# Second layer's sample attention written out with two buffers a side and scores one batch ahead; index key pages fetched in the feed-forward stage before

## What is computed

```python
def dsa_select(qi, wi, q_pos, ki, k_pos, k_sel):
    s = jnp.einsum('bqhd,bkd->bqhk', qi, ki).astype(jnp.float32) * (IDX_DIM ** -0.5)
    score = jnp.einsum('bqhk,bqh->bqk', jax.nn.relu(s), wi.astype(jnp.float32)) * (IDX_HEADS ** -0.5)
    score = jnp.where(k_pos[None, None, :] <= q_pos[None, :, None], score, -jnp.inf)
    _, idx = lax.top_k(score, k_sel)
...
    s = jnp.einsum('bqgrd,bqkgd->bqgrk', qg, k_sel).astype(jnp.float32) * (HEAD_DIM ** -0.5)
    p = jax.nn.softmax(jnp.where(valid[:, :, None, None, :], s, -jnp.inf), axis=-1)
    o = jnp.einsum('bqgrk,bqkgd->bqgrd', p.astype(v_sel.dtype), v_sel)
```

## Time and profile before

| | |
|---|---|
| median of 3 runs | 2020.21 us (2020.12 to 2026.99) |
| the profiled execution, its own time | 2022.86 us |
| its span, first to last instruction | 2021.0 us |
| mean granted TensorE clock | 0.928 |
| PE busy | 1752.4 us (87%) |
| DVE busy | 893.4 us (44%) |
| ACT busy | 563.9 us (28%) |
| POOL busy | 103.8 us (5%) |
| HBM read, written | 190.57 MB, 8.82 MB |

### The profile page before, as it was taken

One profiled execution on the slowest core, in us unless ns is written; L12 is line 12 of the kernel. 1 busy time (PEld: TensorE's weight loads), 2 busy tenths in 40 slices (PEclk: granted clock), 3 DMA queues, 4 the chain that ended last, 5 costly groups with the idle time before them and its releaser, 6 DMA issues. The chain is left out here.

```text
span 2021.0 us, 30720 instructions
## 1 busy us (share of the span) xinstructions
PE 1752.4 (87%) x11710; PEld 1431.7 (71%) x11718; DVE 893.4 (44%) x1662; ACT 563.9 (28%) x1087; POOL 103.8 (5%) x91
## 2 busy tenths in 40 slices
PE   5998798889889999999982596687779999999999
PEld 4786565455579988999772374454448999789987
DVE  4457354555352222322242779995444322222212
ACT  3322364233232211122131222453222322112211
POOL 1322012000000000000000022000000000000000
PEclk9999898999999999999986798797779899999999
DMA  5232302999422322332212120001553232223221
GB/s 172 74 120 78 121 1 86 373 374 342 140 73 69 83 79 78 84 83 78 81 39 53 50 86 21 22 1 46 160 143 85 63 83 78 78 73 81 80 74 63
DMA packets 176269, 200.73 MB, mean 99 GB/s; under 512 B 21546, under 2 KB 130794, under 8 KB 176170
## 3 DMA queue, kind: packets, MB, share of 16 engines
q1 hardware_dynamic: 171498, 193.12, 30.1%
q10 hardware_dynamic: 4592, 6.05, 0.9%
q0 software_dynamic: 80, 0.26, 0.0%
HBM read 190.57 MB, written 8.82 MB: 99 GB/s over the span
## 5 line engine op out<-in xcount | busy, mean ns | idle before, releaser
L206 PE MATMUL ps<-feat_lo,w_hi 128*128 128x288 f32 x1408 | 417.4, 296 | 8.5 <-DVEq L1850 8.5
L208 PE MATMUL ps<-feat_hi,w_hi 128*128 128x288 f32 x1408 | 417.2, 296 | 0.0
L207 PE MATMUL ps<-feat_hi,w_lo 128*128 128x288 f32 x1408 | 416.9, 296 | 0.0
L188 DVE TENSOR_TENSOR w_lo<-w_raw,w_hi 128x2048 fp32r<-128x2048 f32 x96 | 220.2, 2293 | 387.5 <-ACT w_hi L182 387.4
L182 ACT ACTIVATE w_hi<-w_raw 128x2048 fp32r<-128x2048 f32 x96 | 183.8, 1914 | 407.9 <-PE ps L214 357.7
L206 PEld LDWEIGHTS ps<-feat_lo,w_hi 128*128 128x128 f32 x1408 | 266.3, 189 | 9.8 <-DVEq L1850 9.8
L207 PEld LDWEIGHTS ps<-feat_hi,w_lo 128*128 128x128 f32 x1408 | 266.5, 189 | 0.0
L208 PEld LDWEIGHTS ps<-feat_hi,w_hi 128*128 128x128 f32 x1408 | 266.3, 189 | 0.0
L206 PE MATMUL ps<-w_lo,feat_hi 128*128 128x512 f32 (+1 forms) x448 | 181.0, 404 | 18.9 <-DVE p_xn L739 6.6
L208 PE MATMUL ps<-w_hi,feat_hi 128*128 128x512 f32 (+1 forms) x448 | 177.3, 396 | 0.0
L207 PE MATMUL ps<-w_hi,feat_lo 128*128 128x512 f32 (+1 forms) x448 | 177.1, 395 | 0.0
(11 more groups left out here) (276 smaller groups left out, 2376.7 us busy)
## 6 DMA issues: line engine op xcount, KB each, us to landing
s_vslot<-in_cache_l_v_dram SPq DMA_DIRECT2D x64, 512.0 KB, 6.6
s_kslot<-in_cache_l_k_dram SPq DMA_DIRECT2D x56, 512.0 KB, 6.7
w_raw<-in_w_gate_dram SPq DMA_DIRECT2D x44, 512.0 KB, 4.0
w_raw<-in_w_up_dram SPq DMA_DIRECT2D x44, 512.0 KB, 5.2
w_raw<-in_w_in_dram SPq DMA_DIRECT2D x18, 1024.0 KB, 5.3
w_raw<-in_w_down_dram SPq DMA_DIRECT2D x16, 1024.0 KB, 5.1
s_vslot<-in_cache_l_v_dram SPq DMA_DIRECT2D x64, 128.0 KB, 2.7
s_kslot<-in_cache_l_k_dram SPq DMA_DIRECT2D x56, 128.0 KB, 2.1
```

The source lines that it names most:

```text
L188: dve.tensor_tensor(self.K.w_lo[:, n % 2, :], self.K.w_raw[:, n % 2, :], self.K.w_hi[:, n % 2, :].bitcast(F32), ALU.subtract).then_inc(sel ...
L206: pe.matmul(out, lhs[0], rhs[1], start=start, stop=False)
L207: pe.matmul(out, lhs[1], rhs[0], start=False, stop=False)
L208: return pe.matmul(out, lhs[0], rhs[0], start=False, stop=stop)
```

## The change

There are two edits. First, the 64 index pages are fetched in `f0g1`, the second `gate_up` of layer 0, 5 or 6 behind each chunk's weight load on SyncE's queue; `kidx_pages` lives from there to the end of layer 1, with a semaphore that outlives the phase. `project` loses its `aside`. Second, layer 1 no longer calls `sample_attention` but a function of its own, `selected_attention`, whose batches are written out without loops. It has two buffers each for key pages, value pages, turned keys (all in `kt0`), queries, new keys and running sums, two pairs of score banks; the masks and the new values of all batches come with two DMAs at the start. TensorE turns the keys of batch b+2 and scores batch b+1 ahead of weighing batch b. Here is the diff, cut:

```diff
@@ project (pi: parts[:1])
-def project(nc, K, parts, tag, aside=None, side=None):
+def project(nc, K, parts, tag, side=None):
...
             for i, n in enumerate(tiles):
                 W.load_up_to(sp, n + 2)
...
-                if aside is not None:
-                    for j in range(DEC_BATCH * i // len(tiles), DEC_BATCH * (i + 1) // len(tiles)):
-                        aside(sp, j)
@@ gate_up
-def gate_up(nc, K, tag, act_hi, act_lo, first, n_chunks):
+def gate_up(nc, K, tag, act_hi, act_lo, first, n_chunks, pages=None):
...
         def _(sp):
+            if pages is not None:
+                total = DEC_BATCH * N_PAGES
+                for n in range(n_chunks):
+                    W.load_up_to(sp, first + n + 2)
+                    pages.load(sp, total * n // n_chunks, total * (n + 1) // n_chunks)
             W.load_up_to(sp, first + n_chunks + 2)
@@ IndexPages
-        self.landed = K.sem("kidx_pages_landed")
+        self.landed = nc.alloc_semaphore(name="kidx_pages_landed")
-    def load(self, sp, b):
+    def load(self, sp, first, last):
         K = self.K
-        for j in range(N_PAGES):
-            n = b * N_PAGES + j
+        for n in range(first, last):
             pid = sp.value_load(K.pages[0:1, n:n + 1], min_val=0, max_val=K.cache_l1_kidx.shape[0] - 1)
-            sp.dma_start(self.rows[:, b, j, :], K.cache_l1_kidx[ds(pid, 1), :, :]
+            sp.dma_start(self.rows[:, n // N_PAGES, n % N_PAGES, :], K.cache_l1_kidx[ds(pid, 1), :, :]
                          .rearrange("a k d -> (a k) d")).then_inc(self.landed, 16)
@@ ffn, two_layers
-                gate_up(nc, K, f"{tag}g{f}", act_hi, act_lo, gu, FH)
+                gate_up(nc, K, f"{tag}g{f}", act_hi, act_lo, gu, FH, pages if f == 1 else None)
...
-    ffn("f0", ffn0, next_gain=2)
+    second = ExitStack()
+    kidx_pages = IndexPages(nc, K, second)
+    ffn("f0", ffn0, next_gain=2, pages=kidx_pages)
...
-            with ExitStack() as idx:
-                kidx_pages = IndexPages(nc, K, idx)
-                project(nc, K, parts[:1], "pi", aside=kidx_pages.load)
-                score_keys(nc, K, top, sample_top, kidx_pages)
+            project(nc, K, parts[:1], "pi")
+            score_keys(nc, K, top, sample_top, kidx_pages)
...
-        sample_attention(
-            nc, K, "s1", ...)
+        selected_attention(
+            nc, K, K.cache_l1_k.rearrange("n k g d -> n k (g d)"), K.cache_l1_v.rearrange("n k g d -> n k (g d)"),
+            K.s_l1_v, fill_q1, ks, out1_fn, early)
@@ new: selected_attention
+    WIDTH, CHUNKS, UNITS = 256, 2, N_PAGES // 2
...
+        kslot, vslot = (sb(x, [P, 2, N_PAGES, WIDTH]) for x in ("kslot", "vslot"))
+        kt = K.kt0[:, 0:2 * 2 * CHUNKS * BANK].rearrange("p (s g c n) -> p s g c n", s=2, g=2, c=CHUNKS)
...
+        vnew = sb("vnew", [DEC_SEQ, DEC_BATCH, WIDTH])
+        masks = sb("masks", [DEC_SEQ, DEC_BATCH, KEYS], BF16)
...
+            def load_k(b, pages):
+                for j in range(N_PAGES):
+                    if b >= 2:
+                        sp.wait_ge(S["k_turned"], UNITS * (b - 2) + j // 2 + 1)
+                    sp.dma_start(kslot[:, b % 2, j, :], cache_k[ds(pages[j], 1), :, :].rearrange("a k d -> (a k) d"))\
+                      .then_inc(k_in[b % 2][j], 16)
+
+            def load_v(b, pages):
+                if b >= 2:
+                    sp.wait_ge(S["weighed"], b - 1)
+                for j in range(N_PAGES):
+                    sp.dma_start(vslot[:, b % 2, j, :], cache_v[ds(pages[j], 1), :, :].rearrange("a k d -> (a k) d"))\
+                      .then_inc(v_in[b % 2][j // 4], 16)
+
+            sp.dma_start(masks[:, :, :], K.mask_rows.rearrange("b q k -> q b k")).then_inc(S["rows_in"], 16)
+            sp.dma_start(vnew[:, :, :], new_v.rearrange("(b q) d -> q b d", b=B)).then_inc(S["rows_in"], 16)
+            now = ids(1)
+            load_k(1, now)
+            load_v(0, ids(0))
+            load_v(1, now)
+            for b in range(2, B):
+                now = ids(b)
+                load_k(b, now)
+                load_v(b, now)
...
+            for i in range(UNITS):
+                turn_k(0, i)
+            scores(0)
+            for i in range(UNITS):
+                turn_k(1, i)
+            for b in range(B):
+                if b + 1 < B:
+                    scores(b + 1)
+                if b + 2 < B:
+                    turn_k(b + 2, 0)
+                    turn_k(b + 2, 1)
+                turn_probs(b, 0)
+                if b:
+                    turn_o(b - 1)
+                if b + 2 < B:
+                    turn_k(b + 2, 2)
+                turn_probs(b, 1)
+                if b + 2 < B:
+                    turn_k(b + 2, 3)
+                weigh(b)
+            turn_o(B - 1)
...
+            for b in range(B):
+                if b + 2 < B:
+                    kt_out(act, b + 2, 0)
+                probs_out(b)
+                if b + 1 < B:
+                    exp(b + 1, 0)
+                if b + 2 < B:
+                    kt_out(act, b + 2, 2)
+                if b + 1 < B:
+                    exp(b + 1, 1)
+                    exp(b + 1, 2)
...
+            for b in range(B):
+                sums(b)
+                if b + 1 < B:
+                    shift(b + 1)
+                if b + 2 < B:
+                    kt_out(dve, b + 2, 1)
+                if b:
+                    finish(b - 1)
+                if b + 2 < B:
+                    queries(b + 2)
+                probs_out(b)
+                if b + 2 < B:
+                    kt_out(dve, b + 2, 3)
+                o_out(b)
+            finish(B - 1)
```

More of the change, by code:

```diff
@@ L2188, in to, with ffn @@
         return lambda t: prompt[:, c, t * P:(t + 1) * P] if t < PT else sample[:, c, :]
-    def ffn(tag, halves, next_gain=None, store=None):
+    def ffn(tag, halves, next_gain=None, store=None, pages=None):
         with ExitStack() as mem:
@@ L2280, in two_layers @@
     add_product(nc, K, "o0", lambda c, t: feat_lhs(K, c, t), out0, split=True, gain=1, subln=True)
-    ffn("f0", ffn0, next_gain=2)
+    second = ExitStack()
+    kidx_pages = IndexPages(nc, K, second)
+    ffn("f0", ffn0, next_gain=2, pages=kidx_pages)
     renew_semaphores(nc, K)
-    with ExitStack() as layer:
+    with second as layer:
         sb = lambda mem, name, shape: mem.enter_context(nc.sbuf_tensor(name, shape, F32))
```

186 lines of the change are left out of this document (added).

## The result

| | before | after |
|---|---|---|
| median, us | 2020.21 (2019.01 to 2026.99, 5 runs) | 2006.58 (2004.10 to 2014.35, 5 runs) |
| ratio | | 0.9934, 95% [0.9915, 0.9953] |
| profiled execution (its span), us | 2022.86 (2021.0) | 2014.35 (2012.3) |
| second layer's sample attention: `mask_rows` stored to last output copied, us | 126.5 | 154.4 |

The change gains 13.6 us, half of the forecast 27.5, and 2006.6 us lies outside the range of 1981 to 2004. Most of it is there before any part of the change can act differently from them: the weight tile of `pi` leaves at 1057.02 us, in e1 at 1050.18. Its cause was not pursued.

A forecast was written before the change was run, and what follows sets the result against it. SyncE's issue queue was taken to bound the stretch where the change acts; -21.5 and -19 us from moving the index pages and +13 from the new attention sum to -27.5, so 1993 us, range 1981 to 2004.

The forecast's parts named there:

- Part 1: Index page issues moved from `pi` into `f0g1`: -21.5 and -19 us in `pi`, cost 0 in `f0g1`.
- Both stalls of `pi`: ScalarE held 21.57 us by a weight tile queued behind index pages, VectorE 21.5 us at the barrier; both go.
- Rivals B and C: B: only one stall goes, some 2014 us, chance 0.06. C: page issues in `f0g1` delay weight tiles, 2037 us, 0.03.
- Part 2: New attention in layer 1: an added wait on SyncE makes the stage 13 us longer, bounds 9 and 17.
- The ring: In the new attention, SyncE's value issues wait for a weighing that stands behind keys just issued: 17.2 us a cycle.
- rival A: New attention: the wait is already met, SyncE's 12.4 us a batch set the pace; 1964 us in all, chance 0.08.
- The side of the keys, from key issue to value issue: Part of each attention cycle, 8.7 us: key issues, landing of the last page, last key unit, weighing.
- The side of the values and page numbers: Part of each attention cycle on SyncE, 8.5 us: 8 value issues 3.7, 8 page numbers 4.8.
- The end: Attention after `load_v(7)` goes: issues 3.2 us, landing 2.4, second half of the weighing 1.1, output 1.4.
- The start: Attention up to `load_v(2)`, 35.2 us: small DMAs, first page numbers, keys and values, then landing, unit and weighing.
- The clock: TensorE's clock in the attention: about 0.7, so 17.2 us a cycle between 16.6 at full and 17.9 at half.

The follow-up runs named there:

- e1: The change with the old attention called in place of the new one, so only the index pages are moved; 1978.8 us, ratio 0.9801 to the kernel before.
- e3: The change with SyncE issuing the keys of batch b+1 ahead of the values of b; 1972.3 us, ratio 0.9766 to the kernel before.
- e5: The change with TensorE weighing batch b before it turns the keys of b+2, SyncE's order kept; 1982.0 us, ratio 0.9815 to the kernel before.
- e4: The change with TensorE turning the probabilities and the last output before it waits for the keys of b+2; 2000.2 us, ratio 0.9904.
- e8: The change with 30 extra turns of the identity matrix on TensorE just ahead of its wait for the keys; 2006.4 us, ratio 0.9939.
- e10: The change with 66 extra turns of the identity matrix on TensorE just ahead of its wait for the keys; 2000.9 us, ratio 0.9889.
- e7: The change with the value pages and their own page number reads issued from GpSimd's queue; 1950.0 us, ratio 0.9656 to the kernel before.

## Why the prediction was wrong

**Part 1, right.** Both stalls of `pi` went and the page issues in `f0g1` cost nothing: 40.4 us for 40.5. Rivals B and C are refuted by e1. The single steps hold too: ScalarE's split comes directly behind its last ready piece (21.6 us gone, forecast 21.5), the barrier wait is 19.2 us shorter (forecast 19), and the next block starts 0.7 us after ScalarE's last row (forecast 0.9).

**Part 2, mechanism right, size wrong.** The ring was forecast, its place (`load_v(b)` behind the keys of b) and its release (`weigh(b-2)`) are what the trace shows, and e3 and e5 show that it is what costs; rival A, no ring, is refuted. From the first small DMA of the stage to its last row it was forecast 129.3 us long and took 1498.15 - 1353.16 = 145.0. The 15.7 us lie in four terms, of which the first two make the cycle 19.1 us in place of 17.2:

- **The side of the keys, from key issue to value issue: 9.8 us in the mean of five cycles, forecast 8.7**, +5.7. This is the step that failed: landing of the last page, then the last key unit and the weighing. It let TensorE be ready for the last page when it landed. But TensorE cannot start until the first keys are there, 2.8 us after the key issue, and behind them its program has four units, two groups of probabilities and an output to turn before the weighing. In the cycle shown the last page is in by 1417.97 + 5.9 = 1423.9 us, by the forecast's own terms, and TensorE comes to the last unit at 1425.71. That unit and the weighing then take 2.25 us, less than the 2.7 allowed. The forecast's list of what "lies beside" the issues has the scores, the exponentials and the copies; the turns of the probabilities and of the output are in no term of it. In the program they stand behind `turn_k(b + 2, 1)`, and so they wait for the keys too. e4 takes them out of there and gives 8.4 us.
- **The side of the values and page numbers: 9.3 us in the mean, forecast 8.5**, +4.0 in five cycles. Where SyncE had no wait ahead of the values, e3's rows give 1408.62 - 1400.31 = 8.3. Most value issues behind the wait are slower, 4.15 to 4.70 us here, but not all: behind waits of about 6 us, e8 has one of 3.66 at 1401.43 us and e10 one at 1384.73. So the wait alone does not explain it, and the cause stays open.
- **The end, 12.4 us from the last value issue, forecast 8.1**: +4.3. The last landing does not bind there. TensorE still has two batches of probabilities and weighings in a chain, with handovers to ScalarE and VectorE:

```profile
1491.58 1.10 PE L1754 MATMUL ps<-s_vslot,s_pt 128*32 128x64 f32 x64 [0.67 <-DVE s_ptn L1874]
...
1495.57 1.14 PE L1754 MATMUL ps<-s_vslot,s_pt 128*32 128x64 f32 x64 [0.57 <-DVE s_ptn L1874]
...
1497.70 0.45 DVE L2634 COPY att<-ps 64x64 f32<-64x64 f32 x2 [0.39 <-PE ps L1767]
```

  The rows of before already gave 1495.71 to 1507.40, 11.7 us, for the same stretch. I built it from a key page's landing instead.
- The start, `load_v(2)` 36.9 us after the first small DMA where 35.2 was forecast: +1.7, and 1.4 of it is the first time round on the side of the keys (9.98 us from 1380.08).

**The clock.** I took the middle of the two levels; the granted clock was 0.73 in four of five cycles and 0.65 in the last, as the forecast had it (0.7), but the block that counts began at 1.2 GHz each time and stayed there for 3 to 6 us. The Trainium skill ("TensorE: Matmul & The Clock Gate", section "HAM oscillation — how this bites in real kernels") says that bursts between waits for DMA start at the low clock. The trace agrees: behind each wait of 9.2 to 9.5 us for keys, 8 turns take 1.9 to 2.2 us. The forecast's own sum for half clock, 17.9 a cycle, would have been nearer. The failed step and the clock are one cost: at a granted clock of 1.00 the side of the keys takes 8.3 to 8.6 us in e10, with the same turns in it, against 8.1 forecast for full clock. The turns make TensorE late mainly because they run at half clock. It is not the whole miss: e10's cycles are 17.0 to 17.75, against 16.6 forecast for full clock, and 0.5 of these 0.9 us are on the side of the values.

The range took in the clock and a tenth on the issues, but no error in what follows the landing, nor in the end. (The forecast's stage end for full clock, 1516.2, adds up to 1516.8 by its terms; nothing rests on it.)

## What to carry to other kernels

- When two queues or engines wait for each other in order, write down for one cycle every instruction that stands between the waiting one and its release on both, in program order. What can run early must also stand early; e4 moved three steps ahead and gained 1.7 us a cycle.
- A second buffer helps only if the loads ahead of it in the same queue don't need what it waits for. Issue the next keys before the wait (e3, -34 us) or use another queue (e7, -57 us).
- First ask what bounds the queue itself: a register read of a page number cost more here (4.6 / 8 = 0.6 us) than issuing its 128 KB page (0.5), and one edit to where values are issued brought the old attention 24 us, against the rewrite's loss of 30.

## What the runs showed of the hardware

- GpSimd issued a 128 KB page in 4.64 / 8 = 0.58 us, against 0.46 to 0.54 on SyncE in e3 (up to 0.59 in the change); the two queues ran at once and DMAs reached 212 GB/s in the cycle shown, against 110 in the change. The second theory of e7 had allowed over 1 us a page.
- An idle wait of 5.8 us for TensorE was followed by half clock (8 turns in 2.27 us), one of 1.7 us behind 7.4 us of extra turns by full clock (4 in 0.63). The length of the last wait does not decide it alone: in e7 one of 1.9 us, behind two shorter waits and two short bursts, was followed by half clock (4 in 1.08).
